# RMS norm factors as the exponential of a logarithm in place of a square root and a reciprocal

## What is computed

```python
def rms_norm(x, g):
    xf = x.astype(jnp.float32)
    y = xf * lax.rsqrt(jnp.mean(xf * xf, axis=-1, keepdims=True) + NORM_EPS)
    return (y * g.astype(jnp.float32)).astype(x.dtype)
...
        x = x + 0.5 * mx[2] * swiglu_2(modulate(rms_norm_2(x, norm_g[layer, 0]), mx[0], mx[1]),
                                     ffn_w_in[layer, 0], ffn_w_out[layer, 0])
```

## Time and profile before

| | us |
|---|---|
| median of 3 runs | 2753.86 |
| lowest, highest | 2753.29, 2761.36 |
| the profiled execution's own time | 2754.49 |
| its span, from first to last instruction | 2752.7 |
| TensorE busy | 2655.5 |
| VectorE busy | 1713.8 |
| ScalarE busy | 1108.0 |

### The profile page before, as it was taken

How to read it: one execution, slowest core, us unless ns; L and a number is a source line. 1 busy time by engine, 2 the same in 40 slices (tenths; PEclk the granted TensorE clock), 3 DMA queues, 4 the chain that set the end, 5 groups by cost and what they waited for, 6 DMA issues and landing times.

```text
span 2752.7 us, 39891 instructions
## 1 busy us (share of the span) xinstructions
PE 2655.5 (96%) x16424; PEld 2338.3 (85%) x16424; DVE 1713.8 (62%) x2741; ACT 1108.0 (40%) x1745; POOL 0.3 (0%) x5
## 2 busy tenths in 40 slices
PE   6999999999999999999989999999999999998998
PEld 6999899989989998888874688888888888876998
DVE  7566777766768786556651556556665444676655
ACT  5465545545545443322231533223232222355443
POOL 0000000000000000000000000000000000000000
PEclk9999999999999999999999999999999999999999
DMA  4443577634356664445522013445534445331554
GB/s 165 169 143 117 168 234 226 192 130 161 130 168 198 224 214 138 138 149 158 168 69 68 22 65 130 145 152 155 160 121 140 145 150 169 117 115 55 173 180 130
DMA packets 113908, 402.81 MB, mean 146 GB/s; under 512 B 12352, under 2 KB 15552, under 8 KB 113600
## 3 DMA queue, kind: packets, MB, share of 16 engines
q1 hardware_dynamic: 113728, 400.27, 44.9%
HBM read 399.17 MB, written 1.05 MB: 145 GB/s over the span
## 4 chain that ended last, share of the span: by engine, by line
PE 87%; DVE 8%; ACT 3%; issue 1%; DMA 0%; SPq 0%; DVEq 0%; ACTq 0%
PE psum L565 25%; PE psum L566 25%; PE psum L567 25%; PE psum L940 3%; PE psum L974 2%; DVE wlo L1621 1%; ACT whi L1185 1%; DVE R L1662 1%; DVE arena L1662 1%; PE psum L1041 1%; PE psum L1015 1%; DVE arena L1751 1%; PE psum L997 0%; PE psum L985 0%; ACT HHI L1205 0%
## 5 line engine op out<-in xcount | busy, mean ns | idle before, releaser
L565 PE MATMUL psum<-HHI,whi 128*128 128x256 f32 (+1 forms) x3488 | 1121.4, 321 | 34.7 <-DVE wlo L1621 10.9
L566 PE MATMUL psum<-HLO,whi 128*128 128x256 f32 (+1 forms) x3488 | 1107.9, 318 | 0.0
L567 PE MATMUL psum<-HHI,wlo 128*128 128x256 f32 (+1 forms) x3488 | 1107.5, 318 | 0.0
L1621 DVE TENSOR_TENSOR wlo<-wring,whi 128x1024 fp32r<-128x1024 f32 x589 | 706.4, 1222 | 329.8 <-ACT whi L1185 327.6
L1185 ACT ACTIVATE whi<-wring 128x1024 fp32r<-128x1024 f32 x589 | 604.9, 1053 | 384.4 <-PE psum L567 360.8
L565 PEld LDWEIGHTS psum<-HHI,whi 128*128 128x128 f32 x3488 | 671.8, 193 | 90.3 <-issue 16.8
L566 PEld LDWEIGHTS psum<-HLO,whi 128*128 128x128 f32 x3488 | 671.9, 193 | 43.7 <-issue 1.4
L567 PEld LDWEIGHTS psum<-HHI,wlo 128*128 128x128 f32 x3488 | 671.3, 192 | 42.2
L565 PE MATMUL psum<-HIDHI,whi 128*128 128x256 f32 (+1 forms) x1122 | 368.9, 329 | 0.0
L566 PE MATMUL psum<-HIDLO,whi 128*128 128x256 f32 (+1 forms) x1122 | 368.1, 328 | 0.0
L567 PE MATMUL psum<-HIDHI,wlo 128*128 128x256 f32 (+1 forms) x1122 | 368.1, 328 | 0.0
(11 more groups left out here) (301 smaller groups left out, 1984.1 us busy)
## 6 DMA issues: line engine op xcount, KB each, us to landing
wring<-ffn_in SPq DMA_DIRECT2D x264, 512.0 KB, 4.2
wring<-mod_w SPq DMA_DIRECT2D x144, 512.0 KB, 4.3
wring<-ffn_out SPq DMA_DIRECT2D x96, 448.0 KB, 4.0
wring<-w_proj SPq DMA_DIRECT2D x66, 512.0 KB, 4.0
wring<-w_gate SPq DMA_DIRECT2D x64, 512.0 KB, 4.0
wring<-ffn_out SPq DMA_DIRECT2D x48, 512.0 KB, 4.3
wring<-w_up SPq DMA_DIRECT2D x20, 512.0 KB, 3.5
wring<-w_out SPq DMA_DIRECT2D x16, 512.0 KB, 3.5
```

Source lines behind the costliest of these rows:

```text
L565: mm(out_, w[0], a[0], start=start, stop=False)
L566: mm(out_, w[0], a[1], start=False, stop=False)
L567: return mm(out_, w[1], a[0], start=False, stop=stop)
L1621: TTN(wlo[:, i, :], wring[:, raw_slot(tag, k), :], whi[:, i, :].bitcast(F32), ALU.subtract).then_inc(sem("weights_lo"), 1)
```

## The change

`root` becomes `rsqrt`: ScalarE takes the logarithm of sum/count + eps into the same buffer, waits for its own result, and takes the exponential of -0.5 times it in place. VectorE's reciprocals are gone (26 instructions), and VectorE waits for the exponential in place of the root. `root_table` becomes `logarithm_table` at the same places, and is called at two more: in `half_tail` behind the first half's factor and one split, and, in the first block's last FFN, behind the tiles of m = 5.

```diff
-            def root_table():
+            def logarithm_table():
 
-                A(SPARE[:, 0:1], one, ACT.Sqrt)
+                A(SPARE[:, 0:1], one, ACT.Ln)
...
                 half_factor(norm, 0)
                 half_hi(norm, 0, range(2), l, n3)
                 split_ahead(tag, lots_[0])
+                logarithm_table()
                 for t in tiles_[:-1]:
                     act.wait_ge(*done("x_ready", (tag, t)))
                     square_half(norm, 1, t)
...
-            def root(out_, bank_key, n, count, name, key):
+            def rsqrt(out_, bank_key, n, count, name, key):
 
                 act.wait_ge(*done("filled", bank_key))
-                A(flat(out_), bank_of(bank_key)[:, 0:n], ACT.Sqrt, bias=eps, scale=1.0 / count).then_inc(*freed(bank_key, name, key))
+                bank = bank_of(bank_key)
+                out_ = flat(out_)
+
+                A(out_, bank[:, 0:n], ACT.Ln, bias=eps, scale=1.0 / count).then_inc(*freed(bank_key))
+                act.wait_ge(*done("free", bank_key))
+                A(out_, out_, ACT.Exp, scale=-0.5).then_inc(*mark(name, key))
...
                                 half_hi(norm, 1, range(2 * m - 8, 2 * m - 6), 0, 0)
+                                if m == 5:
+                                    logarithm_table()
...
-            def invert(buf):
-                ln(v.reciprocal(buf, buf))
...
                     v.wait_ge(*done("fox_r", (l, 1)))
-                    invert(t1["RF"])
```

More of the change, by code:

```diff
@@ L1199, in half_factor @@
             def half_factor(tag, s_):
-                root(R[:, seqs(s_)], ("ss", tag, s_), SEQ, D, "factor", (tag, s_))
+                rsqrt(R[:, seqs(s_)], ("ss", tag, s_), SEQ, D, "factor", (tag, s_))
             def half_hi(tag, s_, tiles_, l, n3):
@@ L1339, in fox_act @@
                     for i in range(2):
-                        root(t1["RF"][:, 2 * i:2 * i + 2, :], ("ssf", l, i), 512, HD, "fox_r", (l, i))
+                        rsqrt(t1["RF"][:, 2 * i:2 * i + 2, :], ("ssf", l, i), 512, HD, "fox_r", (l, i))
                 if FOX_SCORES <= j < FOX_SCORES + HEADS:
@@ L1381, in gla_act @@
                 gate_step(l, "gss")
-                root(g1["OQ"], ("gss", l), 512, HD, "gla_r", l)
+                rsqrt(g1["OQ"], ("gss", l), 512, HD, "gla_r", l)
             def head_values(l, okey, buf, name):
@@ L1399, in ret_act @@
                 gate_step(l, "rss")
-                root(r1["OQ"], ("rss", l), 512, HD, "ret_r", l)
+                rsqrt(r1["OQ"], ("rss", l), 512, HD, "ret_r", l)
             def ssd_act(l):
@@ L1415, in ssd_act @@
                 gate_step(l, "yss")
-                root(d1["OQ"][:, 0:2, :], ("yss", l), 512, 256, "ssd_r", l)
+                rsqrt(d1["OQ"][:, 0:2, :], ("yss", l), 512, 256, "ssd_r", l)
             def merge_act(l):
@@ L1448, in mla_act @@
                 for part, count in ((0, 512), (1, 256)):
-                    root(b2["RM"][:, part, :], ("mss", part), 512, count, "mla_r", part)
+                    rsqrt(b2["RM"][:, part, :], ("mss", part), 512, count, "mla_r", part)
                 for t in range(12):
@@ L1559, in _ @@
             for l in range(DEPTH):
-                root(R[:, 0:SEQ], ("ss", ("n1", l)), SEQ, D, "factor", ("n1", l))
+                rsqrt(R[:, 0:SEQ], ("ss", ("n1", l)), SEQ, D, "factor", ("n1", l))
                 norm_hi(("n1", l), SEQ)
@@ L1571, in _ @@
                 residual(f"wo{l}", ("n2", l), SEQ)
-                root(R[:, 0:SEQ], ("ss", ("n2", l)), SEQ, D, "factor", ("n2", l))
+                rsqrt(R[:, 0:SEQ], ("ss", ("n2", l)), SEQ, D, "factor", ("n2", l))
                 norm_hi(("n2", l), SEQ)
@@ L1584, in _ @@
                 if l:
-                    root(R[:, 0:n], ("ss", ("b2", l)), n, D, "factor", ("b2", l))
+                    rsqrt(R[:, 0:n], ("ss", ("b2", l)), n, D, "factor", ("b2", l))
                     norm_hi(("b2", l), n, l, 2)
                 ffn(f"ffi2{l}1", f"ffo2{l}1", ("b2", l), n, *((("b0", 1), BOTH) if l == 0 else ("final", SEQ)))
-            root(R[:, 0:SEQ], ("ss", "final"), SEQ, D, "factor", "final")
+            rsqrt(R[:, 0:SEQ], ("ss", "final"), SEQ, D, "factor", "final")
         @block.vector
```

14 lines of the change are left out of this document (3 added, 11 removed).

## The result

The changed kernel takes 2735.69 us (median of 4 runs, 2734.48 to 2737.04); the kernel before took 2755.69 beside it (4 runs, 2753.29 to 2761.36). The ratio is 0.9925, with a 95% interval of 0.9907 to 0.9942. The forecast was 2734.5 with a range of 2729 to 2745. The profiled execution of the changed kernel has a span of 2732.7 where before had 2752.7: 20.0 less.

A forecast was written before the change was run, and what follows sets the result against it. TensorE, busy 2655.5 of 2752.7 us, was taken as the bound, so only its waits counted. Terms 4.4 + 7.9 + 2.9 + 3.4 + 2.5 - 0.8 - 0.9 = 19.4 gave 2735.1, or 2734.5 as a median; range 2729 to 2745.

The forecast's parts named there:

- attention, waits: Attention factors of both layers: scores start at 64.65 instead of 66.83 in layer 0; 2.2 us per layer, 4.4 gained.
- attention, clock: Behind the attention scores of both layers: both falls of the granted clock (4.7 and 3.2) go, 7.9 us gained.
- GLA: GLA's factor, ahead of retention's scores: 1.44 us earlier in both layers, 2.9 gained.
- MLA: MLA's first factor: the whole reciprocal goes, TensorE's wait of 7.47 becomes 4.1, 3.4 us gained.
- whole norms: Factors of whole norms: 0.6 twice, 0.8 at the start, 0.4 before the last FFN, 0.15 elsewhere; 2.5 us gained.
- layer 1's FFN: Layer 1's FFN, m = 4 and 5: 0.7 gained, then a load and one element (1.49) ahead of the splits; 0.8 us lost.
- tails: Three tails of the same form: added loads and elements delay the roundings, 0.3 us each, 0.9 lost.
- behind SSD's factor: SSD's and retention's factors: covered by the gate's lots on TensorE; under 0.2 us a layer left, not counted.
- The local term: The clock behind the attention scores in both layers: falls of 4.7 and 3.2 us gone, 7.9, with bounds 0 and 7.9.
- That the falls stay: Rival, behind the attention scores: the clock still falls, the 7.9 us are missing, 2742.4; chance 0.18.
- That the first block hides its gains: Rival, first block: TensorE comes earlier, then lots are late, as refills and splits pace it; 2750.9 us; chance 0.12.
- That a switch costs more than its row: Rival, at some 24 added loads: ScalarE waits further per load, balance at 0.8, 2765 us at 1.28; chance 0.05.

The follow-up runs named there:

- experiment 5: The kernel before with logarithm and exponential at the factors of 512 columns alone, root and reciprocal kept at the 16 of 256 columns: 2737.45 us, ratio 0.9929.
- experiment 4: The changed kernel with one more load of the root's set in the first attention factor of each layer: 2739.08 us, ratio 0.9931.
- one set: The changed kernel with one table set holding both functions, 24 loads in place of 79: 2706.29 us, ratio 0.9817; run again 2708.00, ratio 0.9823.
- runs 1 and 2: The kernel before with only the attention factors changed: 2748.06 us, ratio 0.9960; the changed kernel with root and reciprocal at these alone: 2744.46, ratio 0.9955.
- run 3: The changed kernel with one more load of the root's set between each factor's logarithm and exponential: 2768.28 us, ratio 1.0038.

## Why the prediction was right, step by step

| term | forecast | what the rows show | the stretches |
|---|---|---|---|
| attention, waits | 4.4 | 2.24 + 2.22 from ScalarE's start to the scores | 7.1 + 5.5 with the clock |
| attention, clock | 7.9 | first to second head 10.77 and 9.23 before, 6.06 twice after: 7.9 | in the line above |
| GLA | 2.9 | 1.84 and 1.83 became 0.40 twice: 2.9 | 2.9 |
| MLA | 3.4 | 7.47 became 4.09: 3.4 | 3.3 |
| whole norms | 2.5 | second norm 2.83 to 2.24 from its root (logarithm) to VectorE's first product with the factor; before the last FFN 4.39 to 3.97; start 7.30 to 5.45 | 0.6 + 0.6 + 0.3 + 1.2 |
| layer 1's FFN | 0.8 lost | 2.68 became 3.47: 0.8; and a fall of the clock | 3.2 lost |
| tails | 0.9 lost | sum of waits unchanged in the first | 0.4, 0.1 and 0.3 lost in the three, 0.1 won behind MLA's product |
| behind SSD's factor | under 0.2 a layer, not counted | from the root (logarithm) to VectorE's first product 4.11 to 2.66; a wait of 0.17 gone | 0.4 + 0.4 |
| clock behind layer 1's second norm | not in the sum | a fall that before's execution lacks | 1.5 lost |
| clock behind MLA | not in the sum | a fall of before's execution gone | 1.6 |
| grouped window attention, layer 1 | not in the sum | a wait of 2.21 for 2.80, the falls at another moment | 1.4 |

The last column sums to 19.9 of the 20.0 between the two spans; everywhere else the two traces agree to 0.05.

**The waits.** Without the clock the terms sum to 11.5; the page has 12.8. The start of the program gave more than the 0.8, since the first input came earlier in this execution; the kernel of experiment 5, which keeps the root there, has 6.56 where before had 7.30. The other terms of the waits were met within 0.3, and each with the mechanism named: distances between rows of the three engines, less 1.28 and an exponential. The estimates for operations that the trace of before didn't have held as well: a logarithm out of a bank takes 0.68 or 0.69 for 512 columns, like the root; the exponential 0.42 for 256 columns; the single element 0.20.

**The clock.** The local term was right to a tenth, and it is the least certain part of the answer. That the sum came so close is luck in part. The step that I had mis-sized is layer 1's FFN: I put 0.8 into the sum and named a possible fall of 1 to 2, and the place lost 3.2.

```profile
985.00:1025.00 40.00, 36.53 (x286) 36.30 (x285) 28.65 (x51) 22.66 (x35) 0.00 (x0) 0.91 0.45 146
```

The same stretch was at 1.00 before. With the 1.5 behind the second norm of layer 1, where the wait is the same 1.78 as before (1.77), 3.9 were lost that the sum doesn't have. On the other side stand 3.8 that it doesn't have either: the 1.6 behind MLA, the 1.4 in layer 1's window attention and the 0.8 behind SSD. The windows at the second place behind MLA, in before and then in after:

```profile
1515.00:1545.00 30.00, 27.42 (x105) 17.68 (x104) 11.63 (x38) 13.61 (x34) 0.00 (x0) 0.94 0.05 18
```

```profile
1498.00:1528.00 30.00, 27.39 (x112) 18.32 (x111) 13.10 (x44) 13.90 (x38) 0.00 (x0) 1.00 0.06 18
```

**What a fall costs in a tail: nothing.** In the tails the clock fell four times before and twice after, but this gave the change no gain, as the kernel with the attention factors alone shows: its tails are the code of before, with the same wait of 2.22 or 2.23, and its clock fell in two of them. The fourth tail in before, with a fall, and then in that kernel, without: the matmul behind the wait, the first one of the next lot, and the granted clock of 15 us around both.

```profile
2395.10 0.58 PE L565 MATMUL psum<-HHI,whi 128*128 128x256 f32 x1 [2.22 <-DVE HLO L1683]
...
2402.31 0.28 PE L565 MATMUL psum<-HHI,whi 128*128 128x256 f32 x1
...
2390.00:2405.00 15.00, 12.78 (x94) 12.53 (x94) 13.47 (x24) 10.00 (x17) 0.00 (x0) 0.89 0.13 36
```

```profile
2388.26 0.39 PE L565 MATMUL psum<-HHI,whi 128*128 128x256 f32 x1 [2.22 <-DVE HLO L1693]
...
2395.38 0.38 PE L565 MATMUL psum<-HHI,whi 128*128 128x256 f32 x1 [0.67 <-DVE wlo L1631]
...
2383.00:2398.00 15.00, 12.11 (x94) 11.53 (x94) 13.73 (x26) 10.03 (x17) 0.00 (x0) 1.00 0.09 31
```

It is 7.21 with the fall and 7.12 without. TensorE goes faster in the second, and then waits 0.67 more for the next lot's subtraction, which VectorE makes behind the roundings. Here VectorE sets the pace, and so less busy time of TensorE is no gain. So the split of the 20.0 into 12.8 of waits and 7.2 of clock says less than it seems: where a fall is gone in a tail, 0.7 of waiting stands in its place. On a row of lots for which TensorE doesn't wait, a fall costs 1.5 (experiment 4).

All tails: TensorE's longest single wait in the first, third and fourth (in the second), the granted clock of 30 us around each, and each as a stretch:

| kernel | longest wait | clock in the four tails | the four stretches |
|---|---|---|---|
| before | 2.23 (1.71) | 0.94, 0.94, 0.94, 0.94 | 46.44, 41.01, 54.62, 41.84 |
| attention factors alone | 2.22 (1.71) | 1.00, 0.94, 0.94, 1.00 | 46.44, 41.03, 54.64, 41.86 |
| factors of 512 columns alone | 2.21 (2.21) | 0.94, 0.94, 0.94, 0.94 | 46.63, 41.20, 54.64, 41.89 |
| one more load at every factor | 2.68 (1.88) | 0.94, 0.94, 0.94, 0.94 | 49.24, 44.00, 57.34, 44.66 |
| no table in the tails | 2.82 (2.81) | 0.94, 0.94, 0.89, 0.94 | 47.71, 42.29, 56.44, 43.14 |
| the change | 1.40 (1.71) | 0.94, 0.94, 1.00, 1.00 | 46.80, 40.91, 54.76, 42.10 |
| all but the attention factors | 1.39 (1.71) | 0.94, 1.00, 0.94, 1.00 | 46.80, 40.87, 54.88, 42.09 |
| no table at m = 5 | 1.40 (1.70) | 1.00, 0.94, 0.94, 1.00 | 46.70, 40.85, 54.88, 42.10 |
| one set | 0.66 (0.67) | 1.00, 1.00, 1.00, 1.00 | 44.44, 38.35, 52.48, 39.82 |

(The kernel of experiment 4 is like the one with all but the attention factors.) The clock falls less often behind shorter waits, from one execution of each kernel; what decides in the middle of this list is not settled by these runs. What the tails take goes by the rows of ScalarE and VectorE, which is what the prediction had priced.

**The rivals.** That the falls stay: no, 1.00 where 0.59 to 0.91 stood. That the first block hides its gains: no, by runs 1 and 2. That a switch costs more than its row: no, 1.28 a load, by run 3. At 0.8 of hidden cost a load the change would have come out even; there is none.

## What to carry to other kernels

A step is worth what it takes on the row to the bound engine, so price its replacement there and let the rest of it stand idle: here 12 of 28 factors gave the whole gain. If two functions alternate, first look whether one table set holds both, and name it, because the automatic choice doesn't; that was worth more than the change itself (28 us against 20). Count a fall of the clock only where TensorE sets the pace, and compare the time between the same two matmuls rather than busy time or the sum of waits. A load asked for early is only needed where the engine has no idle time ahead of the instruction that it serves; elsewhere it runs ahead of that instruction's wait by itself, and asking for it early puts it on somebody's row.

## What the runs showed of the hardware

A table load (1.28) runs ahead of the wait of the instruction that needs it: at MLA it ended 1.54 before. Two loads in a row and a load between two activations leave gaps of 0.01 to 0.02. A reciprocal on VectorE takes 1.75 for 256 and 3.35 for 512 columns, four to five times a product of the same size (0.42 and 0.69), so that an exponential with a load ahead of it (1.91) is faster for 512 columns and no faster for 256 (1.70). And whether the granted clock falls behind a wait of TensorE is open over a wide middle: at the attention scores never behind 0.52 (ten times) and always behind 2.96 and 3.08 (six times), but once in two behind 1.80; behind layer 1's FFN not with 2.68 in before's execution and 2.59 with the attention factors alone, yet with 2.72 where the factors of 512 columns were changed alone and with 1.95 without the table at m = 5, and not with 1.33 or 1.42. What a fall costs depends on who sets the pace: 1.5 where TensorE works without a wait behind it, 3.2 and 4.7 behind the scores, where it lasted longer, and nothing in the tails.
